# Expert 0's gate and up products placed inside the dispatch, its down product ahead of expert 1, and the gate rows of the second residual sent through DRAM

## The reference, cut to what matters

```python
mod = (silu(c) @ w_ada + b_ada)            # shift, scale and gate rows; g2 is the last of six
h2 = x * (1.0 + sc2) + sh2
# router: one group of 4 experts, then the best 2 inside it, weights comb (tokens x 16)
hg = jnp.einsum('td,edf->tef', t, w_gate)  # 1024 -> 512, for each expert
hu = jnp.einsum('td,edf->tef', t, w_up)    # 1024 -> 512
hid = jax.nn.silu(hg) * hu * comb[..., None]
out = jnp.einsum('tef,efd->td', hid, w_down)   # 512 -> 1024
x = layer_norm(ALPHA * x + g2 * out, ln2_g, ln2_b)
```

## Time and profile before

| what | before |
|---|---|
| time, median of 3 (us) | 479.68 (479.35 to 480.42) |
| the profiled execution's own time (us) | 478.24 |
| its span in the profile (us) | 476.5 |
| PE busy | 428.8 us, 90% |
| DVE busy | 209.8 us, 44% |
| ACT busy | 121.0 us, 25% |
| POOL busy | 70.4 us, 15% |
| granted PE clock, mean | 0.98 of full |
| DMA, mean over the span | 324 GB/s |
| queue of SP (q1) | 147.13 MB |
| largest shares of the chain of waits | PE 64%, DMA 22%, DVE 7% |

### The profile page before, as it was taken

The page is one execution under the profiler, slowest core; times in us unless marked ns, Lnnn a source line. Parts: engine busy times, 40 slices in busy tenths (PEclk is TensorE's granted clock), DMA queues, the critical chain, the costliest instruction groups (busy, mean ns, idle before and its releaser), DMA issues.

```text
span 476.5 us, 6299 instructions
## 1 busy us (share of the span) xinstructions
PE 428.8 (90%) x2310; PEld 232.2 (49%) x2310; DVE 209.8 (44%) x421; ACT 121.0 (25%) x242; POOL 70.4 (15%) x68
## 2 busy tenths in 40 slices
PE   2579999999999999899999999998888898899982
PEld 1234555465654448496554455554433444363420
DVE  2650724849563436881100110011143635546877
ACT  2400158784230204553112112121101110121110
POOL 2000015276470124002000000000100000000300
PEclk9979999999999999999999999999999989999996
DMA  8999997682999207787899999999999999999503
GB/s 213 364 386 387 303 387 291 227 303 95 336 386 375 96 0 274 269 315 166 305 409 380 428 428 420 429 426 425 419 424 429 420 424 420 427 416 424 211 1 132
DMA packets 35779, 154.51 MB, mean 324 GB/s; under 512 B 4418, under 2 KB 5250, under 8 KB 27545
## 3 DMA queue, kind: packets, MB, share of 16 engines
q1 hardware_dynamic: 32304, 147.13, 80.1%
q10 hardware_dynamic: 2408, 5.17, 3.0%
q0 software_dynamic: 1024, 1.63, 1.0%
HBM read 151.61 MB, written 7.67 MB: 334 GB/s over the span
## 4 chain that ended last, share of the span: by engine, by line
PE 64%; DMA 22%; DVE 7%; issue 2%; ACT 2%; SPq 1%; POOLq 1%; POOL 0%; DVEq 0%; ACTq 0%
PE PS L1661 13%; DMA ring<-in_ex_w_gate 12%; PE PS L1897 11%; PE PS L1763 9%; DMA ring<-in_ex_w_down 7%; PE PS L1904 6%; PE PS L1940 6%; PE PS L1589 4%; PE PS L1838 3%; DMA ring<-in_w_ada 3%; PE PS L1947 3%; PE PS L1638 2%; PE PS L1695 1%; PE PS L1680 1%; DVE y L1303 1%
## 5 line engine op out<-in xcount | busy, mean ns | idle before, releaser
L1897 PE MATMUL PS<-ring,xs 128*64 128x256 f32 x896 | 102.7, 382 | 6.6 <-DMA ring<-in_ex_w_gate 5.2
L1897 PEld LDWEIGHTS PS<-ring,xs 128*64 128x64 f32 x896 | 62.2, 137 | 45.7 <-issue 17.2
L1661 PE MATMUL PS<-hT,ring 128*128 128x388 f32 x192 | 68.9, 510 | 2.6 <-DVE hT L947 2.6
L1940 PE MATMUL PS<-ring,hTs 128*64 128x512 f32 x224 | 52.6, 613 | 6.3 <-DMA ring<-in_ex_w_down 6.2
L1661 PEld LDWEIGHTS PS<-hT,ring 128*128 128x128 f32 x192 | 37.4, 198 | 32.3 <-issue 9.5
L1232 DVE SCALAR_TENSOR_TENSOR sg<-sg,PS 128x256 f32<-128x256 f32 x14 | 5.9, 421 | 63.4 <-ACT sg L758 62.9
L1940 PEld LDWEIGHTS PS<-ring,hTs 128*64 128x64 f32 x224 | 15.6, 140 | 36.8 <-issue 36.1
L1240 DVE SCALAR_TENSOR_TENSOR hid<-sg,PS 128x256 f32<-128x256 f32 x18 | 10.6, 609 | 47.4 <-PE PS L1897 36.9
L1303 DVE SCALAR_TENSOR_TENSOR y<-PS,comb,y 128x1024 f32<-128x1024 f32 x21 | 26.7, 1276 | 0.0
L1589 PE MATMUL PS<-ring,cond 128*32 128x512 f32 x192 | 24.8, 629 | 2.1 <-DVE cond L874 2.0
L1495 POOL TENSOR_SCALAR gtmp<-gtmp 128x388 f32<-128x388 f32 x8 | 9.7, 1213 | 83.6 <-ACT gtmp L560 83.6
(11 more groups left out here) (282 smaller groups left out, 588.0 us busy)
## 6 DMA issues: line engine op xcount, KB each, us to landing
ring<-in_ex_w_gate SPq DMA_DIRECT2D x16, 2048.0 KB, 17.8
ring<-in_ex_w_up SPq DMA_DIRECT2D x16, 2048.0 KB, 20.2
ring<-in_ex_w_down SPq DMA_DIRECT2D x16, 2048.0 KB, 25.7
ring<-in_w_ada SPq DMA_DIRECT2D x11, 2048.0 KB, 13.2
ring<-in_w_in SPq DMA_DIRECT2D x2, 2048.0 KB, 22.2
ring<-in_w_out SPq DMA_DIRECT2D x2, 2048.0 KB, 10.5
slot_rows<-in_empty SPq DMA_DIRECT2D x1, 3648.0 KB, 25.2
ring<-in_w_ada SPq DMA_DIRECT2D x2, 1024.0 KB, 15.9
```

The lines of the kernel that those rows point to most:

```text
L1661: mm = pe.matmul(PS[:, w % 4, 0:W], wt[:, k, (w % 4) * P:(w % 4 + 1) * P], hT[:, k, :], start=(k == 0), stop=(k == KD - 1))
L1897: mm = pe.matmul(PS[HALF * h:HALF * (h + 1), bank, 0:FE // 2], x(k, HALF), w[:, k, h * (FE // 2):(h + 1) * (FE // 2)], start=(k == 0), sto ...
L1940: mm = pe.matmul(PS[HALF * h:HALF * (h + 1), 3, :], x, w[:, f, h * 512:(h + 1) * 512], start=(f == 0), stop=(f == KF - 1))
```

## The change

Five things are done.

1. PE runs gate and up of expert 0 after dispatch 10 instead of after dispatch 15. Dispatches 11 to 15 follow, then turn 0 and down 0 directly, then gate and up of expert 1; the staggered loop begins with e = 1. ACT's and DVE's lists follow suit.
2. The units are renumbered to g0, u0, d0, g1, u1; from g2 (unit 5) on the numbers are as before.
3. Expert 0 gets its own `sg0` and `hid0`, so that it doesn't touch the places that are still in use.
4. The four `g2_row` pieces on PE and their four copies on ACT are gone. Instead, after dispatch 10, PE waits for `st_row`, transposes the g2 columns in two instructions into 8 rows, DVE copies them to `g2row`, and POOL writes them to a DRAM tensor of 2 x 1024 numbers.
5. In iteration 13 ACT issues two loads that read these rows back into `g2r`, each broadcast to 128 partitions (512 KB each). Those who waited for `g2_sb` wait for `g2_in`.

```diff
         def unit(e, j):
+            if e < 2 and (e == 0 or j < 2):
+                return 3 * e + j
             if j < 2:
-                return j if e == 0 else 3 * e - 1 + j + (e == LAST)
+                return 3 * e - 1 + j + (e == LAST)
...
+            def g2_load():
+                used(act, unit(NE - 2, 0))
+                act.wait_ge(s["g2_out"], 16)
+                for q in range(2):
+                    act.dma_start(g2r[:, q, :], g2_rows[q].partition_broadcast(P)).then_inc(s["g2_in"], 16)
...
             dve.tensor_copy(strow[0:8, :], PS[0:8, 1, 0:P]).then_inc(s["st_row"], 1)
+            dve.wait_ge(s["g2_ps"], 1)
+            dve.tensor_copy(g2row[0:KD, :, :], PS[0:KD, 1, P:3 * P].rearrange("k (q p) -> k q p", p=P)).then_inc(s["g2_row"], 1)
...
             pool.dma_start(t["new_state"], strow[0:2 * CR, :]).then_inc(s["st_out"], 16)
+            pool.wait_ge(s["g2_row"], 1)
+            pool.dma_start(g2_rows.rearrange("q (k p) -> k q p", p=P), g2row[0:KD, :, :]).then_inc(s["g2_out"], 16)
...
             def project_out(e):
                 v = unit(e, 2)
                 pe.wait_ge(s["hts_done"], e + 1)
+                if e == 0:
+                    pe.wait_ge(s["disp_sb"], 2 * KD)
...
+            for n in range(4, 2 * KD):
+                dispatch(n)
...
+                if n == KD + 2:
+                    pe.wait_ge(s["st_row"], 1)
+                    for q in range(2):
+                        mm = pe.transpose(PS[0:KD, 1, (1 + q) * P:(2 + q) * P], modT[:, G2 * KD:(G2 + 1) * KD, q], ident)
+                    mm.then_inc(s["g2_ps"], 1)
+                    pe.wait_ge(s["route_done"], 1)
+                    counts[0] = tokens_of(pe, 0)
+                    project_in(0, 0)
+                    project_in(0, 1)
+
+            turn(0)
+            project_out(0)
+            project_in(1, 0)
+            project_in(1, 1)
             most = most_of(pe)
-            for e in range(LAST - 1):
+            for e in range(1, LAST - 1):
                 project_in(e + 1, 0)
...
-                if e == G2_AT:
-                    g2_row(0)
                 turn(e)
```

More of the change, by code:

```diff
@@ L145, in build @@
         strow = at("strow", place[0], [P, P])
+        g2row = at("g2row", place[0] + P * 4, [P, 2, P])
         mrow = keep("mrow", [P, 512])
@@ L207, in build @@
         hid = at("hid", A0 + 36864, [P, FE])
+        sg0 = at("sg0", A0 + 26624, [P, FE])
+        hid0 = at("hid0", A0 + 28672, [P, FE])
         hTs = at("hTs", A0 + 38912, [P, KF, CAP])
@@ L413, in halves, with gated @@
             return v.rearrange("p (a n) -> p a n", n=512)
+        def gated(e):
+            return (sg0, hid0) if e == 0 else (sg, hid)
         def y_parts(e):
@@ L685, in x_out @@
                 act.copy(dst, PS[:, 4 + n % 4, 0:HS]).then_inc(s["disp_sb"], 1)
[L687 to L700, removed]
             counts, offs = {}, {}
@@ L756, in gate_tanh @@
                 need(act, "hid_done", e)
+                g = gated(e)[0]
                 fork(act, counts[e],
-                     lambda: act.activation(sg[:, 0:FE // 2], PS[:, gate_bank(e), 0:FE // 2], ACT.Tanh, scale=0.5)
+                     lambda: act.activation(g[:, 0:FE // 2], PS[:, gate_bank(e), 0:FE // 2], ACT.Tanh, scale=0.5)
                      .then_inc(s["sg_done"], 1),
-                     lambda: act.activation(sg[:, :], PS[:, gate_bank(e), :], ACT.Tanh, scale=0.5).then_inc(s["sg_done"], 1))
+                     lambda: act.activation(g[:, :], PS[:, gate_bank(e), :], ACT.Tanh, scale=0.5).then_inc(s["sg_done"], 1))
             def hid_out(e):
@@ L783, in y_out @@
                      lambda: act.copy(dst[:, :], PS[:, 3:5, :].rearrange("p a n -> p (a n)")).then_inc(s["yh_done"], 1))
-            counts[0] = tokens_of(act, 0)
-            offs[0] = act.value_load(cnt[0:1, 1 + NE:2 + NE], min_val=0, max_val=NSLOT)
-            x_in(1)
[L788 to L794, removed]
+            def g2_load():
[3 more added lines that the diff above has]
+                    act.dma_start(g2r[:, q, :], g2_rows[q].partition_broadcast(P)).then_inc(s["g2_in"], 16)
@@ new lines, in _ @@
+            act.wait_ge(s["x1n"], NT + 1)
+            for n in range(2 * KD):
+                if n == KD // 2:
+                    act.wait_ge(s["prow_ps"], 1)
+                    act.copy(Prow[:, :, :], PS[:, 0:2, 0:TOK]).then_inc(s["prow_sb"], 1)
+                    act.wait_ge(s["x1_done"], NT)
+                x_out(n)
+                if n == KD + 2:
+                    act.wait_ge(s["route_done"], 1)
+                    counts[0] = tokens_of(act, 0)
+                    offs[0] = act.value_load(cnt[0:1, 1 + NE:2 + NE], min_val=0, max_val=NSLOT)
+                    gate_tanh(0)
+                if n == KD + 1:
+                    act.wait_ge(s["gap_done"], 1)
+                    act.activation(mark5[:, :, 2 * NG:3 * NG], mark5[:, :, NG:2 * NG], ACT.Exp).then_inc(s["pos_pool"], 1)
+                    act.activation(rs[:, 9, :], rs[:, 8, :], ACT.Exp).then_inc(s["pos_pool"], 1)
@@ L796, in _ @@
+            hid_out(0)
+            x_in(1)
+            rows_out(0)
+            gate_tanh(1)
+            x_in(2)
             most = most_of(act)
-            for e in range(LAST - 1):
+            for e in range(1, LAST - 1):
                 gate_tanh(e + 1)
                 if e == G2_AT:
-                    g2_copy(0)
+                    g2_load()
                 hid_out(e)
-                if e == G2_AT:
-                    g2_copy(1)
                 x_in(e + 2)
-                if e == G2_AT:
-                    g2_copy(2)
@@ L1249, in hidden @@
                 need(dve, "ht_ps", e)
-                fork(dve, counts[e], lambda: hid_part(up_bank(e), 0).then_inc(s["hid_done"], 1),
-                     lambda: (hid_part(up_bank(e), 0), hid_part(up_bank(e), 1).then_inc(s["hid_done"], 1)))
+                fork(dve, counts[e], lambda: hid_part(up_bank(e), 0, e).then_inc(s["hid_done"], 1),
+                     lambda: (hid_part(up_bank(e), 0, e), hid_part(up_bank(e), 1, e).then_inc(s["hid_done"], 1)))
             def choose(e):
@@ L1317, in slot_marks @@
                 dve.wait_ge(s["st_out"], 16)
+                dve.wait_ge(s["g2_out"], 16)
                 dve.wait_ge(s["modT_ps"], COL_COUNT[GE])
@@ L1334, in slot_gates @@
                 dve.wait_ge(s["ab_sb"], 1)
[L1335 removed]
+                dve.wait_ge(s["g2_in"], 32)
                 used(dve, unit(LAST - 1, 1))
@@ L1856, in _ @@
             counts = {}
[L1857 to L1866, removed]
             def project_in(e, j, ks=range(KD)):
@@ L1883, in project_in @@
                     need(pe, "hid_done", e)
+                    if e == 0:
+                        pe.wait_ge(s["g2_row"], 1)
                 loaded(pe, v)
@@ L2030, in slot_weights @@
                 fork(pe, counts[LAST], lambda: tiles(HALF), lambda: tiles(P))
[L2032 to L2042, removed]
+            for n in range(4, 2 * KD):
+                dispatch(n)
+                if n == KD:
+                    pe.wait_ge(s["prow_sb"], 1)
+                    ada_cols(GE)
+                    pe.wait_ge(s["state_done"], 8)
+                    pe.transpose(PS[0:8, 1, 0:P], stin[:, 0:8], ident).then_inc(s["st_ps"], 1)
+                if n == KD + 2:
+                    pe.wait_ge(s["st_row"], 1)
[10 more added lines that the diff above has]
+            project_in(1, 1)
             most = most_of(pe)
-            for e in range(LAST - 1):
+            for e in range(1, LAST - 1):
                 project_in(e + 1, 0)
```

26 lines of the change are left out of this document (10 added, 16 removed).

## The result

The changed kernel needs 485.86 us (median of 7, 481.65 to 486.53) against 479.68 us. The ratio is 1.0102, 95% interval 1.0074 to 1.013, so it is slower by 4.9 us (3.6 to 6.2). The two medians alone lie 6.2 us apart, at the upper edge of that interval. The range 481.0 to 486.8 holds the median, which lies 2.2 us above the forecast of 483.7. The profiled execution is the quickest of the seven, 481.65 us with a span of 479.9.

A forecast was written before the change was run, and what follows sets the result against it. The expert stage was taken as bound by the full-rate weight stream behind an uneven start. Lag 4.4 plus drag 1.2 less 1.6 given back made +4.0 us, 483.7 on the median of 479.68, range 481.0 to 486.8.

The forecast's parts named there:

- Two questions, the start of the stream and the way to the end: Expert stage: when the weight stream reaches full rate for good, and how long from its late landings to the end.
- Gate 0 at 215.2, done at 222.1, up at 228.9: PE, expert 0 inside the dispatch: gate starts at 215.2 instead of 219.05; units 7 and 8 issue 4.0 us earlier.
- Down 0 ends at 243.1: PE after the dispatches and turn 0: down 0 starts at 236.0, after about 1.3 us for the copy, and needs 7.07.
- Unit 9 issued 6.5 us later, landing at 250.8: SP's weight loads: unit 9 waits for down 0's slot until 243.1, needs 7.7 us, lands at 250.8 against 246.4.
- fixed part of 2.8: Lone weight load: 7.7 us, of which 4.9 are its 2.1 MB at 424 GB/s and 2.8 a fixed part.
- A lag of 4.4 that isn't made up: Weight stream from unit 9 on: 4.4 us late to the end, the rate being at its ceiling; bounds 3.3 to 5.4.
- Drag of the g2 loads 1.2 ahead of down 13: Two g2 loads, 1 MB, on ACT's queue take 1.2 us from the stream ahead of down 13; bounds 0 to 2.5.
- 1.6 given back, since down 13 waits for its landing next: PE at down 13: removing the g2 pieces gives back at most 1.6 us, not 3.3; its weight load limits next.
- The sum, +4.0: Whole kernel: lag 4.4 plus drag 1.2 less 1.6 gives +4.0 us on the profiled 478.24, 482.2; median 483.7.
- early issue of units 7 and 8: Rival, stream start: it keeps the 4.0 us won by units 7 and 8; end moves by -4.4 to 475.3; chance 0.08.
- The lag was not absorbed: Rival, stream start: unit 7's early start saves 2.5 us, lag about 2, end +0.4 without drag, 480.1; chance 0.08.
- The g2 rows came in time: Rival: g2 rows reach DVE late for `slot_gates` at about 445.0; after 24 us, +4.7 beyond the sum, 488.4; chance 0.12.

The follow-up runs named there:

- hold9: The kernel before, with SP issuing the loads of units 9 and 10 only when down 0 is done: +8.6 us against the kernel before.
- kept_order: The changed kernel with units numbered as before and PE's loop staggered from expert 0 on: +3.7 us against the kernel before.
- after_again: The changed kernel as it is, run and profiled once more: +4.0 us against the kernel before.
- after_third: The changed kernel as it is, a third time: +2.4 us against the kernel before.
- moved_only: The kernel before with only expert 0's products moved and units renumbered, g2 rows still made on PE: +4.9 us against the kernel before.
- after_busy: The changed kernel with 8 idle matmuls in front of down 13 and 4 behind it, results unused: +1.9 us against the kernel before.
- kept_tight: kept_order with gate 0 behind dispatch 12, its count read earlier, and ACT reading expert 1's numbers before its last two copies: +1.9 us against the kernel before.
- after_tight: The changed kernel with gate 0 behind dispatch 12 and its count read one dispatch earlier: +1.9 us against the kernel before.
- g2_only_again: Repeat of the kernel before with only the g2 rows sent through DRAM, expert 0 and units unchanged: -0.8 us against the kernel before.
- g2_busy: The kernel before with g2 rows through DRAM and 12 idle matmuls about down 13: -1.1 us against the kernel before.

## Why the prediction was right, and where it was off

1. *Two questions, the start of the stream and the way to the end.* Right. `hold9` turns 11.2 us of late issue, 10.2 of late landing, into 9.0 us of late end. A small misreading stands beside it: the low slice of the earlier trace rows with 166 GB/s is the one from 214 to 226 us, not 226 to 238.
2. *Gate 0 at 215.2, done at 222.1, up at 228.9.* Measured 215.4, 222.6, 229.4. The wait for the state row and the read were 0.17 and 0.83 us.
3. *Down 0 ends at 243.1.* Measured 243.0. PE idled 0.86 us between turn 0 and down 0, where I had taken 1.3; gate 0 started 0.2 later than I had it.
4. *Unit 9 issued 6.5 us later, landing at 250.8.* Issued at 243.1, landed at 251.9: it needed 8.8 us and not 7.7. In the nine profiles where it starts behind a hole it needed 8.6 to 9.0. ACT's two row writes of 256 KB, issued 1.3 us behind it in the changed kernel, are not the reason, for `kept_order` has 8.7 without them in its flight. The fixed part of 2.8 that I took from units 7 and 8 is thus not fixed: unit 8 took 7.4 to 8.1 in thirteen profiles and 9.9 in `hold9`. One thing goes with it: in each flight of unit 9 behind a hole lies one packet of the instruction queue (q8) that takes 0.9 us; in the thirteen shorter flights of unit 8 none does before their last 0.3 us, and in the one of 9.9 us one does. It fits, but no run tried it. The 2.0 us that the prediction sets beside its 2.8 is stated by the Trainium skill ("DMA: Bandwidth & Descriptors", Anatomy of one DMA) for DMAs issued from GpSimd; these units go out on SP's queue, and in the five profiles in which it is issued at 243.0 or 243.1, unit 9 lands at 251.7 at the earliest, not at 250.0.
5. *A lag of 4.4 that isn't made up.* Measured 4.2 at gate 14, and 4.3, 4.1, 4.4 and 4.4 in `after_again`, `after_third`, `moved_only` and `after_busy`. The queue behind unit 9 swallowed the extra us of point 4: unit 9 is 5.5 late, unit 12 4.5. In between the lag isn't constant (3.1 at unit 20).
6. *Drag of the g2 loads 1.2 ahead of down 13.* Mis-sized. Down 13 lags 4.7 with them, and in `moved_only`, without them, 4.0 (430.9 against 426.9): 0.5 to 0.7. From gate 14 to down 13 the lag changes by +0.27 us in the mean of the ten profiles with the loads and by -0.35 in that of the four without: 0.6. The row that I had and set aside, 60 GB/s from the 19.0 us broadcast, gave 0.6. The loads landed after 9.2 and 14.8 us.
7. *1.6 given back, since down 13 waits for its landing next.* Right: down 13 starts 0.4 behind its landing and 3.0 us late, where the lag alone is 4.7. `moved_only` against the changed kernel has 4.5 against 3.0 at this place.
8. *The sum, +4.0.* With the drag as measured it is 4.2 + 0.5 - 1.6 = 3.1, and `after_busy`, the profile of this order that also has the g2 loads and no low clock in the tail, gives 3.3. The timed runs gave 4.9, 4.0 and 2.4. So that the forecast of +4.0 lies so near to them is in part luck: the drag was taken 0.6 too large, and the clock, worth about 1 us by the estimate above, was left out. That term I had not at all: I read 1.00 in the stretch from 360 to 380 and did not ask where it was lower. The profile of before that I summed against was a cheap one, with its low clock at 380; one in the tail costs 1.3 to 2 us.

The rivals: the early issue of units 7 and 8 gave nothing, since the hole moved behind them. The lag was not absorbed. The g2 rows came in time, at 438.4 for DVE's use at 442.65; in `after_again` only 1.4 us were left. The room of at least 4 us that the prediction gives the loads behind down 13 shrank too, since behind the two g2 loads they land 6.8 us late and PE is only 3.0 late: d14 lands 2.3 us ahead of its use in the changed kernel, against 5.7 before.

What the forecast didn't see, although it didn't hurt the number, is the second thing that gate and up 0 did behind the dispatch: they covered ACT's gathering for expert 1. In the changed kernel down 0 took that over. `kept_order` showed what it costs without: 2.47 us.

## What to carry to other kernels

Where a stream of loads runs at its ceiling to the end, what a reordering is worth is read from the issue times of the first loads behind the reordered work: not the first one that comes earlier, but the last one that comes later, and such a hole is paid nearly in full, less the time that the late load stood in the queue before. Before moving work, list what it covered: here it hid one engine's gathering and a copy between two products, 0.86 to 2.47 us each. The same holds for work that is taken away: without the g2 pieces PE's mean clock is lower, and part of the gain is gone. And sum against a profile only after looking where its clock was low; a halved clock costs nothing where the engine waits anyway, and 1.3 to 2 us where it doesn't.

## What the runs showed of the hardware

- The granted clock of PE falls to half for about 3.4 us at a time, at places that differ from one execution of the same kernel to the next (380 and 438.7 in two of before; three places between 420 and 470 in `after_again`, the second one 6.8 us long). A group of 16 matmuls that needs 3.65 us then needs 4.92 to 5.67.
- The part up to the mark, in which the kernels do the same work, took 198.0 to 200.8 us in their profiles.
- A read of a token count with nothing queued ahead leaves PE idle for 0.83 to 0.88 us (changed kernel, `kept_order`); read two dispatches earlier it leaves no idle time (`kept_tight`, `after_tight`).
- A 2 MB load into an idle queue put its first packet out about 1.0 us after its issue. The down unit 7 then landed after 7.7 us in three profiles (the kernel before, `g2_only_again`, `g2_busy`) and 8.3 to 9.5 in three others; the up unit 9 behind a hole after 8.6 to 9.0 in nine.
- Two 512 KB broadcasts from DRAM beside the stream landed after 9.2 and 14.8 us (8.9 to 10.2 and 14.5 to 16.1 in ten profiles) and delayed the load under way by 0.5 to 0.7 us, and the next one, down 14, by 2.3 (6.8 late in the changed kernel, 4.4 in `moved_only`): about the whole 1 MB at the stream's 424 GB/s, which is 2.5 us.
- Over 83 executions without the g2 pieces on PE its mean granted clock was 0.9829, over 112 with them 0.9857.
